# A diffusion layer on eight cores: the residual stream kept in an HBM scratch during the MLP, longer contractions, and no arithmetic on GpSimd there

## The chip, the cores and the metric

The kernel runs on the eight cores of one Trainium2 chip. Each pair of cores takes one of the four batch elements and each core of a pair one half of its 2048 tokens, so each core computes 1024 tokens of the output. The time is that of the slowest core, in device microseconds (us).

## The reference, cut to what matters

```python
D_MODEL = 2048; D_FF = 8192; BATCH = 4; SEQ = 2048     # float32

def hybrid_layer(...):                       # depth 1
    h = modulate(rmsnorm(x, g1), sh1, sc1)
    q, k, v, u = split_proj(h @ w_in)        # 12 query heads, 4 kv heads, 4 Fourier groups
    ...                                      # attention over 256 context + 2048 latent keys
    x = x + gt1 * (concat([attn, four]) @ w_out)
    h2 = modulate(rmsnorm(x, g2), sh2, sc2)
    a = relu(h2 @ w1)                        # (2048 -> 8192)
    x = x + gt2 * ((a * a) @ w2)             # (8192 -> 2048)
return rmsnorm(x, final_norm_g)
```

The case is about the last lines: the squared-ReLU MLP and the residual `x` to which it is added.

## The kernel before

Everything is held transposed: features on the 128 partitions, tokens along the free dimension, in two token groups `tg` of 512. The residual stream of a core, 16 feature tiles `d` by two token groups of [128, 512] in float32, is called `ACC(tg, d)` and lives in SBUF as the tiles `acc_0`, `acc_1` (tg 0) and `acc_2` (tg 1), 8 MB in all. The output projection (`w_out`) adds to it; the sum of its squares gives the second norm, whose result, in bf16, is `h_0`, `h_1`, `h_2`.

The MLP then runs as a list of units. The 8192 hidden features are 32 pairs of 256. The first two pairs (weights `wc`) and the second product of the last four pairs (weights `w2l`) are done plainly. All else uses a Strassen-Winograd scheme on 2x2 blocks: seven products take the place of eight. An `Up` unit makes the hidden activations of one pair: its 2x2 blocks are halves of the 2048 input features by the two feature tiles of the pair and by the two token groups, and each of its seven products is 8 matmuls deep, 56 matmuls of 128x128 by 128x512. A `Down` unit makes four output tiles, `(0, d)`, `(1, d)`, `(0, d+8)`, `(1, d+8)`, from one group of `kh` pairs: 7 x kh matmuls. The groups are `GROUPS = [6, 6, 6, 5, 5, 4]` pairs: after the Ups of a group (only those beyond the two plain pairs in the first) come its eight Down units; the last group of four is done plainly at the end by `stage_b`, followed by the final norm and the stores of the output.

A unit `n` has three PSUM banks, `P`, `Q`, `R`, of two sets that take turns, and two of four weight tiles `wr` (`WRAW`), each filled by one DMA on GpSimd's queue that casts float32 to bf16. `sums()` computes five sums of weight blocks on VectorE (three into `ws` tiles, two in place in `wr`). `first()` does two products, of which P is copied by ScalarE to a temporary `s` and Q added to it by VectorE. `mid()` does three products, with P and Q accumulating on; `last()` the remaining two, and it is issued after the next unit's `first()`, except at a turn from Up to Down, where it goes ahead of it since the Down unit needs what the last Up makes. After an Up pair VectorE also forms five sums of the activations (`a2_sums`, over the tiles `a_0` to `a_6`). A temporary comes from `temp()`, which hands out seven tiles in turn (`tt`, `bv`, `cf`, `sqa`).

In a Down unit `take_r` makes four scaled copies on ScalarE (`put`) and adds them to the residual on GpSimd, and `take_12`, `take_21`, `take_11`, `take_22` each add one scaled PSUM bank to a residual tile with one VectorE instruction (`scalar_tensor_tensor`, line 159, with the gate `modcol` or its negative `ng`):

```python
def put(self, acc, col, src, tmp):
    R.act(tmp, src, AF.Copy, scale=col)
    R.tt(acc, acc, tmp, ALU.add, eng='pool')
```

The weights of the last stage, `w2l`, go to parts of the `a` tiles and of `hs_a` that come free, in eight DMAs from the fourth-last unit on.

The order on each engine is not the order of the code: a recorder (`Rec`) collects all operations with the ranges that they read and write, a list scheduler with assumed durations, DMA rates and the priority of the code's order places them, and each engine then executes its own list in that order, with semaphore waits. In the profile most instructions therefore have the line of the recorder's helper: 116 is a matmul, 147 and 170 ScalarE, 156 a tensor_tensor of VectorE or GpSimd, 159 the scalar_tensor_tensor, 182 a DMA.

Of the kernel before, what the change touches and what calls it, by code (L numbers as in the profile page):

```python
# [14 lines left out]
D = 2048  # L15
# [16 lines left out]
class Rec:  # L32
# [47 lines left out]
    def add(self, eng, fn, reads=(), writes=(), dur=0.1, dma=None, nbytes=0, level=None, after=()):  # L80
        r = [x for a in reads for x in self.spans(a)]
        w = [x for a in writes for x in self.spans(a)]
# [338 lines left out]
GROUPS = [6, 6, 6, 5, 5, 4]  # L421
# [31 lines left out]
def build_program():  # L453
# [25 lines left out]
    ccsc_d = din("dft_ch", [128, 256])  # L479
    out_d = nc.dram_tensor("out", [2 * 16 * 128, 512], F32, kind="ExternalOutput").ap()  # L480

    with ExitStack() as st:
# [47 lines left out]
        def at(name, kb, shape, dt=F32):  # L530
# [526 lines left out]
        R.level = 3  # L1057
        h0, h21 = H20, H21[1]
# [20 lines left out]
        def a2_sums(j):  # L1079
            b11, b22, b12, b21, s1, s2, s3 = [A2[c][:, j, :] for c in range(7)]  # L1080
# [10 lines left out]
        for tg in range(2):  # L1091
            for p in range(2):
                for f in range(2):
# [3 lines left out]
                    squared(A2[((0, 3), (2, 1))[tg][f]][:, p, :], PS[b], TT[(0, 3, 6)[rot('tc', 3)]])  # L1097
# [4 lines left out]
        for p in range(2):  # L1102
            a2_sums(p)
# [347 lines left out]
```

How the kernel before makes its waits and increments, by code:

```python
        def run(name, eng):  # L375
            for op in per[name]:
                for kind, a, b, q in op['waits']:
                    if kind == 1:
                        eng.wait_ge(esem[a], self.sig[q])
                    else:
                        eng.wait_ge(dsem[a], b)
                ins = op['fn'](eng)
                if op['dma'] is not None:
                    ins.then_inc(dsem[op['dma']], 16)
                elif op['i'] in self.sig:
                    ins.then_inc(esem[name], 1)
            if name == 'sp':
                for k, v in self.dma_cnt.items():
                    if k.startswith('out'):
                        eng.wait_ge(dsem[k], v)
```

## Time and profile before

| | us |
|---|---|
| median of 3 runs | 1818.13 |
| lowest and highest of them | 1596.5, 1822.4 |
| the profiled execution | 1595.7 |
| its span, on its slowest core (2) | 1594.2 |
| spans of the eight cores | 1581.2 to 1594.2 |

| engine, core 2 | busy us | share |
|---|---|---|
| TensorE matmul (PE) | 1452.7 | 91% |
| VectorE (DVE) | 963.8 | 60% |
| ScalarE (ACT) | 803.8 | 50% |
| GpSimd (POOL) | 387.8 | 24% |

The span of a core is the time from its first to its last instruction; the time of the execution has 1.5 us more. An engine's busy time doesn't tell whether it is what the others wait for: that is in the waits and in the timeline. The MLP begins at 740 us with the matmuls of the `wc` tiles; its units end at 1524 us, where `stage_b` starts.

### The profile page before, as it was taken

Reading aid. Unit: us, or ns where it says so; the run is one execution under the profiler, and the core shown is the slowest. Engines: PE = TensorE matmul, PEld = TensorE weight load, DVE = VectorE, ACT = ScalarE, POOL = GpSimd, SP = SyncE. Lnnn points to the kernel's source line nnn. Section 1 sums busy time; section 2 is a strip of 40 time slices with the busy share of each in tenths; the row PEclk is TensorE's granted clock in tenths of the full one; section 3 lists DMA queues with packets and bytes.
Section 4 is the critical chain, followed back from the end, with each engine's and each line's share of the span. In section 5 each row is a group of like instructions: output and inputs, shape, how many; then the busy total and the mean of one; then the engine's idle time right before and its main releaser. Section 6 shows DMA issues by size and latency. Waiting matters only on the chain.

```text
span 1594.2 us, 29287 instructions; the slowest of 8 cores (1581.2 to 1594.2 us)
## 1 busy us (share of the span) xinstructions
PE 1452.7 (91%) x9931; PEld 752.4 (47%) x10103; DVE 963.8 (60%) x1715; ACT 803.8 (50%) x1706; POOL 387.8 (24%) x467
## 2 busy tenths in 40 slices
PE   0589998989999999999999999999999979979997
PEld 0244554456666666444444444444444434434447
DVE  0253658845445432254777677776776788679447
ACT  1055647567777787154543354334433433443478
POOL 1100010000000010322036304620661354056132
PEclk9989999999999999999999999999999989999999
DMA  9999997479557699005336544555455346446916
GB/s 208 187 192 236 207 166 133 81 128 159 109 95 135 122 189 233 10 14 93 50 56 97 88 92 71 92 91 85 71 87 91 55 67 101 82 58 86 155 21 212
DMA packets 47937, 179.57 MB, mean 113 GB/s; under 512 B 4656, under 2 KB 12208, under 8 KB 37040
## 3 DMA queue, kind: packets, MB, share of 16 engines
q0 software_dynamic: 33584, 139.65, 53.4%
q1 hardware_dynamic: 14208, 38.04, 7.4%
q8 instruction: 84, 1.38, 0.3%
q14 instruction: 61, 0.50, 0.1%
HBM read 308.92 MB, written 8.39 MB: 199 GB/s over the span
## 4 chain that ended last, share of the span: by engine, by line
PE 68%; DMA 19%; DVE 5%; issue 5%; ACT 2%; POOL 1%; another core or an unknown queue 0%; DVEq 0%; ACTq 0%; POOLq 0%; SPq 0%
PE ps L116 67%; DMA wr<-w 6%; DMA wada<-w_ada 5%; DMA xs<-xt 3%; DMA wadb<-w_ada 2%; DVE ws L156 2%; DMA wadm<-w_ada 2%; DVE acc L159 1%; DMA ropeq<-rope_q 1%; POOL acc L156 1%; PE ps L128 1%; DVE hf L156 0%; DVE tt L156 0%; POOL wr L182 0%
## 5 line engine op out<-in xcount | busy, mean ns | idle before, releaser
L147 ACT ACTIVATE pt<-ps 128x512 bf16<-128x512 f32 x432 | 224.0, 633 | 58.5 <-PE ps L116 58.1
L116 PE MATMUL ps<-a,wr 128*128 128x512 bf16 x880 | 204.1, 381 | 14.3 <-DVE acc L159 13.6
L182 POOL DMA_DIRECT2D wr<-w x140 | 76.8, 549 | 449.7 <-DVE tt L156 154.9
L159 DVE SCALAR_TENSOR_TENSOR acc<-ps,modcol,acc 128x512 f32<-128x512 f32 (+2 forms) x176 | 112.2, 650 | 119.0 <-PE ps L116 98.1
L116 PE MATMUL ps<-a,ws 128*128 128x512 bf16 x657 | 157.9, 386 | 21.9 <-DVE ws L156 20.6
L116 PE MATMUL ps<-v,pt 128*128 128x129 bf16 x1728 | 151.8, 220 | 2.7 <-issue 0.6
L116 PEld LDWEIGHTS ps<-a,wr 128*128 128x128 bf16 x896 | 87.5, 98 | 123.0 <-issue 21.1
L116 PEld LDWEIGHTS ps<-v,pt 128*128 128x128 bf16 x1728 | 123.4, 98 | 39.7 <-issue 2.4
L116 PE MATMUL ps<-qT,kT 128*128 128x512 bf16 x385 | 135.3, 381 | 1.0 <-issue 0.2
L156 DVE TENSOR_TENSOR ws<-wr,wr 128x1024 bf16<-128x1024 bf16 (+2 forms) x140 | 105.4, 791 | 44.7 <-DMA wr<-w 41.4
L156 POOL TENSOR_TENSOR acc<-acc,tt 128x512 f32<-128x512 f32 x91 | 118.2, 1309 | 14.7 <-ACT tt L147 13.9
L116 PEld LDWEIGHTS ps<-a,ws 128*128 128x128 bf16 x672 | 65.6, 99 | 105.8 <-issue 32.9
L116 PE MATMUL ps<-h,wr 128*128 128x512 bf16 x472 | 109.6, 380 | 0.5
L116 PE MATMUL ps<-h,ws 128*128 128x512 bf16 x469 | 107.9, 379 | 0.9 <-DVE sqa L156 0.3
L156 DVE TENSOR_TENSOR wr<-wr,wr 128x1024 bf16<-128x1024 bf16 (+2 forms) x140 | 103.8, 778 | 1.0
L116 PE MATMUL ps<-wq,h 128*128 128x512 bf16 x370 | 91.9, 385 | 2.5 <-DVE yk L159 1.7
L116 PE MATMUL ps<-qT,wo 128*128 128x512 bf16 x375 | 87.5, 379 | 0.5
L147 ACT ACTIVATE tt<-tt 128x512 f32<-128x512 f32 x69 | 43.4, 628 | 86.3 <-DVE tt L156 86.2
L156 DVE TENSOR_TENSOR ws<-wr 128x1024 bf16<-128x1024 bf16 (+2 forms) x70 | 72.9, 1041 | 17.5 <-DMA wr<-w 16.9
L116 PE MATMUL ps<-wv,h 128*128 128x512 bf16 x244 | 68.2, 427 | 15.6 <-DMA wv<-w_v 10.6
L147 ACT ACTIVATE sqn<-acc 128x512 bf16<-128x512 f32 (+2 forms) x93 | 42.9, 478 | 76.9 <-DVE acc L159 76.8
L170 ACT COPY tt<-ps 128x512 f32<-128x512 f32 x60 | 34.7, 579 | 89.1 <-PE ps L116 89.1
(240 smaller groups left out, 2382.7 us busy)
## 6 DMA issues: line engine op xcount, KB each, us to landing
wr<-w POOLq DMA_DIRECT2D x60, 512.0 KB, 6.3
wadb<-w_ada POOLq DMA_DIRECT2D x25, 1024.0 KB, 11.7
xs<-xt SPq DMA_DIRECT2D x18, 1024.0 KB, 15.3
wr<-w POOLq DMA_DIRECT2D x48, 384.0 KB, 5.2
wr<-w POOLq DMA_DIRECT2D x32, 320.0 KB, 4.5
wada<-w_ada POOLq DMA_DIRECT2D x8, 1024.0 KB, 36.0
wada<-w_ada POOLq DMA_DIRECT2D x16, 512.0 KB, 13.5
wo<-w_out POOLq DMA_DIRECT2D x8, 1024.0 KB, 11.8
```

The lines of the kernel that those rows point to most:

```text
L116: ins = e.matmul(o, lhsT=l, rhs=r, start=a, stop=b, skip_group_check=more)
L128: ins = e.transpose(out=o, in_=i_, identity=ident)
L147: self.add('act', lambda e: e.activation(out=out, in_=in_, func=func, scale=scale, **kw), reads, writes, dur, level=level)
L156: self.add(eng, lambda e: e.tensor_tensor(out=out, in0=a, in1=b, op=op), [a, b], [out], dur, level=level)
L159: self.add('dve', lambda e: e.scalar_tensor_tensor(out=out, in0=a, scalar=s, in1=b, op0=op0, op1=op1), [a, b] + ([] if isinstance(s, float ...
L170: self.add('act', lambda e: e.copy(out=out, in_=in_), [in_], [out], 0.051 + self.fs(in_) / 1.2e3, level=level)
L182: return self.add(q, lambda e: e.dma_start(out=out, in_=in_), [] if load else [in_], [out] if load else [], 0.55 if q == 'pool' else 0.45, ...
```

## The change

Before the MLP the eight quarters of the residual (4 tiles each, 1 MB) are stored by DMAs of SyncE's queue to a scratch in HBM, `mid`. Each Down unit fetches its four residual tiles from there with four DMAs of 256 KB (`fetch`, into the tiles `ar`, two sets of four) and stores them back with four others (`keep`), all on SyncE's queue; the last group of Downs fetches them straight to where the last stage wants them (`accf`) and stores nothing. `take_r` is now four VectorE instructions that add the scaled bank R and the temporary `s` to the fetched tiles; ScalarE's four copies and GpSimd's four additions are gone. The SBUF that this frees makes the groups longer, `[10, 9, 9, 4]`: 24 Down units in place of 40, with the same number of matmuls. The Ups of the last four pairs now come ahead of the last group of Downs, with activations in places of their own (`PL`), so that the stage after the Downs follows them directly; there are two turns from Up to Down in place of five. `w2l` is loaded by seven DMAs, four of them during the last Downs and three (10 of the 16 blocks) behind the last unit.

```diff
-GROUPS = [6, 6, 6, 5, 5, 4]
+GROUPS = [10, 9, 9, 4]
...
+    mid_d = nc.dram_tensor("mid", [32 * 128, 512], F32, kind="Internal").ap()
...
-        HSA = at('hs_a', 44, [8, 512], BF16)
-        HS1 = at('hs_1', 52, [8, 512], BF16)
-        HS2 = at('hs_2', 36, [8, 512], BF16)
+        HSA = at('hs_a', 144, [8, 512], BF16)
+        HS1 = at('hs_1', 152, [8, 512], BF16)
+        HS2 = at('hs_2', 176, [8, 512], BF16)
...
-        A2 = [at('a2_%d' % i, kb, [KH, 512], BF16) for i, kb in enumerate((76, 82, 88, 94, 100, 60, 66))]
+        A2 = [at('a2_%d' % i, kb, [KH, 512], BF16) for i, kb in enumerate((76, 86, 96, 42, 108, 118, 128))]
...
+        W2L = [at('wl_%d' % i, kb, [n, 8, 128], BF16) for i, (kb, n) in enumerate(((140, 2), (200, 2), (138, 1), (190, 1), (76, 4), (86, 4), (108, 2)))]
+        AR = [at('ar_%d' % i, 60 + 2 * i, [512]) for i in range(8)]
...
         R.level = 3
+        for tg in range(2):
+            for d in (8, 12, 0, 4):
+                src = A1[:, d:d + 4, :] if tg else A0[d // 8][:, d % 8:d % 8 + 4, :]
+                R.dma('sp', mid_d[(tg * 16 + d) * 128:(tg * 16 + d + 4) * 128, :].rearrange("(g p) n -> p g n", p=128),
+                      src, 'ms%d_%d' % (tg, d), load=False, far=((), range(tg * 16 + d, tg * 16 + d + 4)))
...
         class Down(Unit):
...
-            def put(self, acc, col, src, tmp):
-                R.act(tmp, src, AF.Copy, scale=col)
-                R.tt(acc, acc, tmp, ALU.add, eng='pool')
+            def fetch(self):
+                for i, (tg, d) in enumerate(self.spots):
+                    t = tg * 16 + d
+                    R.dma('sp', self.at[i], rows(mid_d, t), 'al%d' % t if self.end else 'ar%d' % (self.n % 2 * 4 + i), far=((t,), ()))
...
+            def take(self, i, c, src):
+                R.stt(self.at[i], src, self.col[c], self.at[i], ALU.mult, ALU.add)
 
             def take_r(self):
-                self.put(ACC(1, d), ncol(d), self.s, temp())
...
+                self.take(0, 0, self.R)
+                self.take(3, 1, self.R)
+                self.take(1, 2, self.s)
+                self.take(2, 3, self.s)
 
             def take_12(self):
-                self.take(ACC(1, self.d), gcol(self.d), self.P)
+                self.take(1, 0, self.P)
+                self.keep(1)
...
-            turn = i and spec[0] is Down and units[i - 1][0] is Up
+            turn = i and spec[0] is Down and units[i - 1][0] is Up and i < len(units) - 8
...
-            for k in {len(units) - 4: (0, 1), len(units) - 3: (2, 3, 4), len(units) - 2: (5, 6)}.get(i, ()):
-                load_late(k, [sent])
+            if i >= len(units) - 5 and i < len(units) - 1:
+                load_late(i - len(units) + 5, [sent])
             u.mid()
             if i + 1 < len(units):
                 made[i + 1].sums()
+                if units[i + 1][0] is Down:
+                    made[i + 1].fetch()
             load(i + 2, 0)
+        for k in (4, 5, 6):
+            load_late(k)
         made[len(units) - 1].last()
```

How the order of three engines changes. GpSimd, at the end of the first Downs, before: four additions to the residual stand between the weight DMAs of each unit.

```order
L182 DMA wr_169<-w 128x1536
L182 DMA wr_172<-w 128x1536
L156 TENSOR_TENSOR acc_157<-acc_157,sqa 128x512
L156 TENSOR_TENSOR acc_156<-acc_156,bv 128x512
L156 TENSOR_TENSOR acc_155<-acc_155,tt_184 128x512
L156 TENSOR_TENSOR acc_157<-acc_157,cf 128x512
L182 DMA wr_171<-w 128x1536
L182 DMA wr_170<-w 128x1536
```

The same queue in the changed kernel, where the first Downs begin:

```order
L182 DMA wr_169<-w 128x2560
L182 DMA wr_172<-w 128x2048
L182 DMA wr_171<-w 128x2560
L182 DMA wr_170<-w 128x2560
L182 DMA wr_172<-w 128x2560
```

Only DMAs are left, of 10 blocks (2560 elements a partition) in place of 6.

VectorE, one Down unit before: five weight sums of 768 elements, the addition of Q to `s` and four takes.

```order
L156 TENSOR_TENSOR ws_176<-wr_171 128x768
L156 TENSOR_TENSOR ws_174<-wr_169,wr_170 128x768
L156 TENSOR_TENSOR ws_175<-wr_170,wr_169 128x768
L156 TENSOR_TENSOR wr_170<-wr_169,wr_170 128x768 x2
L156 TENSOR_TENSOR cf<-cf,ps 128x512
L159 SCALAR_TENSOR_TENSOR acc_155<-ps,ng,acc_155 128x512
L159 SCALAR_TENSOR_TENSOR acc_157<-ps,ng,acc_157 128x512
L159 SCALAR_TENSOR_TENSOR acc_157<-ps,modcol,acc_157 128x512
L159 SCALAR_TENSOR_TENSOR acc_156<-ps,modcol,acc_156 128x512
```

And in the changed kernel:

```order
L156 TENSOR_TENSOR ws_176<-wr_171 128x1280
L156 TENSOR_TENSOR ws_174<-wr_169,wr_170 128x1280
L156 TENSOR_TENSOR ws_175<-wr_170,wr_169 128x1280
L156 TENSOR_TENSOR wr_170<-wr_169,wr_170 128x1280 x2
L156 TENSOR_TENSOR cf<-cf,ps 128x512
L159 SCALAR_TENSOR_TENSOR ar_198<-cf,ng,ar_198 128x512
L159 SCALAR_TENSOR_TENSOR ar_201<-ps,ng,ar_201 128x512
L159 SCALAR_TENSOR_TENSOR ar_199<-cf,ng,ar_199 128x512
L159 SCALAR_TENSOR_TENSOR ar_204<-ps,ng,ar_204 128x512
L159 SCALAR_TENSOR_TENSOR ar_197<-ps,modcol,ar_197 128x512
L159 SCALAR_TENSOR_TENSOR ar_200<-ps,modcol,ar_200 128x512
L159 SCALAR_TENSOR_TENSOR ar_198<-ps,modcol,ar_198 128x512
```

The takes go to the fetched tiles `ar`, and there are eight of them in a unit, two of which read the temporary (`cf` here) and not a bank.

SyncE's queue between the loads of the residual and the stores of the output, before:

```order
L182 DMA acc_156<-xo 128x2048 [waits s_dve]
L182 DMA acc_155<-xo 128x2048 [waits d_adb1_0,s_pe]
L182 DMA acc_157<-xo 128x2048 [waits s_pe] x3
L182 DMA acc_155<-xo 128x2048 [waits d_adb0_0,s_pe]
L182 DMA out<-acc_155 128x4x512 [waits s_dve]
```

Nothing stands between them.

The same queue in the changed kernel, in the middle of the first Downs (`s_dve` is a wait for VectorE, `d_as0` to `d_as7` one for the end of the store of that residual tile):

```order
L182 DMA mid<-ar_197 128x512 [waits s_dve]
L182 DMA mid<-ar_200 128x512 [waits s_dve]
L182 DMA mid<-ar_202 128x512 [waits s_dve]
L182 DMA ar_197<-mid 128x512 [waits d_as0]
L182 DMA mid<-ar_203 128x512 [waits s_dve]
L182 DMA ar_200<-mid 128x512 [waits d_as3]
L182 DMA ar_202<-mid 128x512 [waits d_as5]
L182 DMA ar_203<-mid 128x512 [waits d_as6]
```

Each tile is stored when its last take is done, and the same SBUF tile is fetched anew, for the next unit but one, when its store has ended; fetches stand in the queue behind stores that wait for VectorE.

## Rows read from the trace of the kernel before

**Rows 1.** Windows: length, busy us by engine, clock, DMA share, GB/s; the MLP.

```profile
740.00:826.00 86.00, 84.84 (x388) 38.54 (x395) 59.92 (x102) 49.65 (x81) 6.50 (x11) 1.00 0.30 46
826.00:1524.00 698.00, 652.96 (x2926) 291.30 (x2983) 511.07 (x761) 277.81 (x453) 276.09 (x294) 0.99 0.53 86
1524.00:1594.00 70.00, 61.98 (x560) 43.23 (x563) 43.03 (x83) 54.97 (x142) 25.69 (x25) 0.96 0.37 121
```

**Rows 2.** Windows of 50 us inside the MLP; columns as above.

```profile
1200.00:1250.00 50.00, 49.79 (x229) 22.65 (x233) 32.27 (x59) 23.24 (x40) 5.05 (x10) 1.00 0.51 88
1250.00:1300.00 50.00, 40.68 (x177) 17.79 (x180) 38.50 (x54) 19.55 (x33) 24.45 (x24) 0.93 0.41 59
1300.00:1350.00 50.00, 43.88 (x192) 19.12 (x195) 45.04 (x54) 16.02 (x25) 25.60 (x26) 0.97 0.55 86
...
1400.00:1450.00 50.00, 42.19 (x183) 18.48 (x185) 40.75 (x55) 19.23 (x30) 33.77 (x32) 0.93 0.44 62
1450.00:1500.00 50.00, 44.84 (x197) 19.62 (x199) 35.92 (x46) 18.14 (x29) 20.19 (x25) 0.97 0.82 124
```

**Rows 3.** Timeline of PE: start, length, operation, count [idle before, releaser].

```profile
776.71 1.89 PE L116 MATMUL ps<-hs_a,wr 128*128 128x512 bf16 x8
...
788.80 1.89 PE L116 MATMUL ps<-hs_a,wr 128*128 128x512 bf16 x8
...
830.49 2.75 PE L116 MATMUL ps<-a,wr 128*128 128x512 bf16 x12 [1.77 <-DVE acc L159]
...
1284.37 4.08 PE L116 MATMUL ps<-a,ws 128*128 128x512 bf16 x10 [6.29 <-DVE ws L156]
```

**Rows 4.** Waits of PE, 740 to 1524 us: us in total, times, longest.

```profile
PE ps L116 <- DVE ws L156: 20.6, 9, 6.3
PE ps L116 <- DVE acc L159: 15.6, 12, 3.6
...
PE ps L116 <- DMA wr<-w: 2.3, 1, 2.3
```

**Rows 5.** Timeline of DVE; columns as for PE.

```profile
1262.84 5.30 DVE L156 TENSOR_TENSOR wr<-wr,wr 128x640 bf16<-128x640 bf16 x1
...
1270.05 2.07 DVE L159 SCALAR_TENSOR_TENSOR acc<-ps,modcol,acc 128x512 f32<-128x512 f32 x3
```

**Rows 6.** Timeline of POOL over the same moments.

```profile
1262.84 1.29 POOL L156 TENSOR_TENSOR acc<-acc,tt 128x512 f32<-128x512 f32 x1
1264.07 1.28 POOL L156 TENSOR_TENSOR acc<-acc,sqa 128x512 f32<-128x512 f32 x1
1265.30 1.26 POOL L156 TENSOR_TENSOR acc<-acc,tt 128x512 f32<-128x512 f32 x1
1266.53 1.25 POOL L156 TENSOR_TENSOR acc<-acc,cf 128x512 f32<-128x512 f32 x1
```

**Rows 7.** Groups by form: 830 to 1480 us, then Ups (1205 to 1250).

```profile
L159 DVE SCALAR_TENSOR_TENSOR acc<-ps,modcol,acc 128x512 f32<-128x512 f32 x80 | 58.2, 745 | 30.3 <-POOL acc L156 20.1 <-PE ps L116 10.2
...
L156 DVE TENSOR_TENSOR wr<-wr,wr 128x640 bf16<-128x640 bf16 x32 | 32.4, 1048 | 0.2
...
L156 DVE TENSOR_TENSOR wr<-wr,wr 128x1024 bf16<-128x1024 bf16 x8 | 5.1, 685 | 0.0
```

**Rows 8.** DMA queues: packets, MB, share; 826 to 1480, then 1560 to 1594.

```profile
q0 software_dynamic: 17756, 52.68, 50.1%
...
q1 hardware_dynamic: 8448, 8.39, 73.8%
...
out<-acc SPq DMA_DIRECT2D x8, 256.0 KB, 2.6
```

**Rows 9.** The two weight DMAs of 1 MB (tile wc).

```profile
L182 POOL DMA_DIRECT2D wc<-w x2: 530/550/570, 711.8 to 712.9; - x2
...
DMA to landing us min/median/max: 11.1/12.6/14.2
```

**Rows 10.** DMA share in 40 slices of the span (page).

```profile
DMA  9999997479557699005336544555455346446916
```

More of the change, by code:

```diff
@@ L77, in spans, with add @@
         return out
-    def add(self, eng, fn, reads=(), writes=(), dur=0.1, dma=None, nbytes=0, level=None, after=()):
-        r = [x for a in reads for x in self.spans(a)]
-        w = [x for a in writes for x in self.spans(a)]
+    def add(self, eng, fn, reads=(), writes=(), dur=0.1, dma=None, nbytes=0, level=None, after=(), far=((), ())):
+        r = [x for a in reads for x in self.spans(a)] + [('D', i, i + 1) for i in far[0]]
+        w = [x for a in writes for x in self.spans(a)] + [('D', i, i + 1) for i in far[1]]
         i = len(self.ops)
@@ L1077, in squared, with slots, a2_sums @@
             R.act(dst, tmp, AF.Square)
-        def a2_sums(j):
-            b11, b22, b12, b21, s1, s2, s3 = [A2[c][:, j, :] for c in range(7)]
+        def slots(j):
+            return [A2[c][:, j, :] for c in range(7)]
+        def a2_sums(of):
+            b11, b22, b12, b21, s1, s2, s3 = of
             R.tt(s2, b11, b12, ALU.add)
@@ L1102, in build_program @@
         for p in range(2):
-            a2_sums(p)
+            a2_sums(slots(p))
         class Unit:
@@ new lines, in __init__ @@
+                self.end = g == len(GROUPS) - 2
+                self.at = [ACCF(*k) if self.end else AR[n % 2 * 4 + i] for i, k in enumerate(self.spots)]
+                self.col = [f(d + 8 * i) for f in (gcol, ncol) for i in range(2)]
+            def fetch(self):
+                for i, (tg, d) in enumerate(self.spots):
+                    t = tg * 16 + d
+                    R.dma('sp', self.at[i], rows(mid_d, t), 'al%d' % t if self.end else 'ar%d' % (self.n % 2 * 4 + i), far=((t,), ()))
@@ new lines, in keep @@
+            def keep(self, i):
+                if not self.end:
+                    tg, d = self.spots[i]
+                    t = tg * 16 + d
+                    R.dma('sp', rows(mid_d, t), self.at[i], 'as%d' % (self.n % 2 * 4 + i), load=False, far=((), (t,)))
+            def take(self, i, c, src):
+                R.stt(self.at[i], src, self.col[c], self.at[i], ALU.mult, ALU.add)
+            def take_r(self):
+                self.take(0, 0, self.R)
+                self.take(3, 1, self.R)
+                self.take(1, 2, self.s)
+                self.take(2, 3, self.s)
@@ L1214, in take_22 @@
             def take_22(self):
[L1215 removed]
+                self.take(3, 3, self.Q)
+                self.keep(3)
         units = []
@@ L1219, in build_program @@
         for g, size in enumerate(GROUPS):
+            plain = g == len(GROUPS) - 1
             for j in range(size):
                 if base + j > 1:
-                    units.append((Up, base + j, j))
+                    units.append((Up, base + j, PL[4 * j:4 * j + 4] if plain else slots(j)))
             base += size
-            if g < len(GROUPS) - 1:
+            if g < len(GROUPS) - 2:
                 units += [(Down, g, d, size) for d in range(8)]
+        units += [(Down, len(GROUPS) - 2, d, GROUPS[-2]) for d in range(8)]
         made = {}
@@ L1232, in load @@
                 return made[i].load(half)
-        late_w = [(0, 3, flat(A2[4][:, 0:6, :])), (3, 6, flat(A2[5][:, 0:6, :])), (6, 9, flat(A2[6][:, 0:6, :]))]
-        late_w += [(9 + c, 10 + c, flat(A2[c][:, 4:6, :])) for c in range(4)] + [(13, 16, flat(HSA[:, 0:6, :]))]
         def load_late(k, after=()):
-            lo, hi, dst = late_w[k]
-            R.dma('pool', dst, w2l_d[:, 1024 * lo:1024 * hi], 'wl%d' % k, after=after)
+            lo = sum(w.shape[1] for w in W2L[:k])
+            n = W2L[k].shape[1]
+            R.dma('pool', W2L[k].rearrange("p d j n -> p (d j n)"), w2l_d[:, 1024 * lo:1024 * (lo + n)], 'wl%d' % k, after=after)
         for i in range(2):
```

68 lines of the change are left out of this document (33 added, 35 removed).

## The prediction

> **What bounds the kernel now.** I read the windows of the MLP first, then the timeline and the waits of PE, then what VectorE and GpSimd did in the longest of them, last the DMA queues. In the MLP's units, 740 to 1524 us, PE is busy 84.8 + 653.0 of 784 us [rows 1]. One Up unit, 56 matmuls, takes 788.80 - 776.71 = 12.09 us where nothing disturbs it [rows 3], 0.216 us a matmul. The units have 128 + 30 x 56 + 8 x 7 x 28 = 3376 matmuls, 729 us at that pace. So 784 - 729 = 55 us are lost, and that is all that a change which keeps the matmuls can win there. The reader should see where they lie: a stretch of Ups loses next to nothing (49.79 of 50 us), the windows with the Downs of 5 pairs lose 9.3 and 7.8 us of 50 in idle time, and in these the granted clock falls to 0.93 [rows 2]: after an idle time of 6.29 us, 10 matmuls take 4.08 us in place of 2.16 [rows 3], so part of them ran at the lower of the two levels, 1.2 GHz.
>
> PE waits 20.6 us for weight sums (`ws`) and 15.6 us for the takes (`acc`), which must empty a bank [rows 4]. Both are VectorE's. Why is it late? At 1262.84 us a weight sum of 640 elements takes 5.30 us [rows 5], and at the same 1262.84 GpSimd begins four additions to the residual, back to back until 1267.78 [rows 6]. The sums in place of this form average 1048 ns in the Downs, while those of 1024 elements take 685 ns in the Ups, where GpSimd adds nothing [rows 7]. A bf16 sum on VectorE is held up by GpSimd's additions, for as long as they follow one another. That is the bound that the change touches.
>
> **What goes.** (1) The additions, and with them the 36.2 us of waits for VectorE. (2) The slow clock behind them: (1 - granted clock) x 50 us is 3.5, 1.5 and 3.5 us in the windows from 1250, 1300 and 1400 [rows 2], 8.5 us. (3) The wait of 2.3 us for a weight DMA and the 1.5 us of slow clock in the window from 1450 [rows 2, 4]: there `w2l` is loaded between the weights, at a DMA share of 0.82. Now one DMA of it comes in each of the last units, of a kind that needs less, and I count 3.8 us as won. ScalarE's four copies go too; nothing on PE waits for them. Together 48.5 us. Of the 55 the other 6.6 are small waits and the matmuls' own jitter, and I leave them.
>
> **What comes on VectorE.** A Down unit of 10 pairs has 70 matmuls, 15.1 us of PE; of 9 pairs 63, 13.6 us. VectorE has in it five sums of 1280 elements: 8 sums of 1024 took 5.1 us [rows 7], 0.64 each, so 0.80 each and 4.0 in all; one addition, 0.7; and eight takes in place of four, at the pace of three in 2.07 us [rows 5] 5.5 us. That is 10.2 of 15.1 us, 67% (9.8 of 13.6, 72%, with 9 pairs). In the Ups, VectorE is busy 32.27 of 50 us, 65%, and PE waits for nothing [rows 2]. So the added takes are hidden as long as nothing blocks VectorE. At a turn VectorE does cost: the first one has a wait of 1.77 us [rows 3]. Two turns are left; I give back 2 us each, 4 in all (0 to 10).
>
> **What comes on the DMA engines.** The weight queue moved 52.68 MB at a share of 50.1% of 654 us, that is 6.2 us of all 16 engines for each MB that it writes [rows 8]. SyncE's queue moved 8.39 MB in 73.8% of 34.2 us, 3.0 us a MB [rows 8]. A Down unit of 10 pairs needs 1.31 MB of weights (8.2 us) and 1.05 MB of residual each way (6.3 us): 14.5 us in the 15.1 that PE takes. Of 9 pairs: 7.3 + 6.3 = 13.6 of 13.6. The last group, which stores nothing, needs 7.3 + 3.2 and 1.2 for `w2l`. So in the first 16 Downs the DMA engines, at 0.53 now [rows 1], are filled to 96 and 100%. This is the new risk, and it is carried by what is fetched ahead: a weight DMA has 8 to 12 products (17 to 26 us) between its issue and its use, a fetch of the residual about 10 us, behind two stores. Then VectorE has three more products before PE needs the bank. A 256 KB transfer lands in 2.6 us when alone [rows 8]. What it lands in beside a full weight queue the trace doesn't show. From below the cost is 0, since the demand still fits; from above, were every MB of residual as dear as one of weights, a unit of 10 would need 8.2 + 13.1 = 21.3 us and one of 9 20.4, 8 x 6.2 + 8 x 6.8 = 104 us too much. I take 6 us, near the lower end, since the tail's row is of the very transfer (same queue, 2 KB rows, all cores at once) and the average fits.
>
> The eight stores of the residual before the MLP, 8.39 MB or 25 us of DMA time, fall where the DMA share is 0 for two slices, 80 us [rows 10], and stand ahead of nothing on SyncE's queue until the first fetch. I cost them at nothing; if the last of them were late it would be the first `a2_sums`, whose tiles lie on `acc_2`, and 5 us at most.
>
> Behind the last unit: 2.6 MB of `w2l` are issued in the order 2, 4, 4 blocks, the one needed first last. Before, two DMAs of 1 MB issued at 711.8 and 712.9 landed within 14.2 us [rows 9], 2 MB in 15.3. So 2.6 MB land some 18.5 us after the end of product m1. PE has two products of that unit's middle, two of its end (4 x 1.9) and six blocks (6 x 8 x 0.216 = 10.4) before it needs them, 18.1 us. I take 1 us (0 to 6).
>
> **The sum**, against the profiled execution's own 1595.7 us (span 1594.2 and 1.5 around it; 0.8 under the lowest of the three timed runs, and far under their median of 1818.13, since two of the three took over 1818; the forecast is for an execution like the profiled one): 1595.7 - 48.5 + 4 + 6 + 1 = 1558.2, taken as 1558. That is 2.4% less. A measurement of this kernel can tell about 2% from no change, 1564 us, so the forecast lies close to that line.
>
> One rule of the Trainium skill speaks against the change. The page SBUF — State Buffer, section The DMA setup-cost knee, gives a transfer of 256 KiB 224 GB/s where one of 1 MiB gets 341, because each pays about 2 us that don't scale. The rows above have 332 GB/s for a queue whose transfers were 256 KB to 1 MB, because several were under way. By the rule 2.1 MB of residual take 9.4 us, a unit of 10 needs 17.5 us in 15.1, and the time comes to that of the second rival.
>
> **Rivals.** (a) *The additions weren't the cause.* Then VectorE stays late for want of time, with four more takes. Against it: 5.30 us for one sum, to the moment of GpSimd's run. Time: 36.2 + 8.5 stay, 1558 + 45 = 1603. 5%.
>
> (b) *The DMA engines become the bound, in part*: the residual costs not 3.0 but 4.5 us a MB beside weights. Then a unit of 10 needs 8.2 + 9.4 = 17.6 us, one of 9 16.7: 8 x 2.5 + 8 x 3.1 = 45 us in place of my 6, 1597; half of that, 1577. For it: no margin at all in the second group. Against: the price per MB of either queue. 27%, from 1566 to 1600.
>
> (c) *Slower: the residual's transfers run one after the other.* SyncE's queue is in order, and each fetch waits for a store, which waits for VectorE. Eight transfers of 2.6 us are 20.8 us a unit. If they don't overlap, VectorE waits for each unit's tiles, PE for the banks: 8 x (20.8 - 15.1) + 8 x (20.8 - 13.6) = 103 us, 1655. It decides from 15.1 / 8 = 1.9 us a transfer on. Against it: the order has up to four of them back to back. 11%.
>
> (d) *Everything fits*: no DMA cost, no turn cost, 1547 or just under. 5% beyond the range below it.
>
> The forecast itself, 1547 to 1566, has 52%. From 1564 up to 1600, (a) in part and (b), about a third. So: faster by over 2% 0.56, within 2% 0.32, slower 0.12. The range of 8 in 10 is 1546 to 1600: it leaves out (c), most of (a) and what lies under 1546.
>
> **What would show it.** In the profile after: bf16 sums of 1280 elements near 0.85 us in the Downs, none over 1.5; no additions on GpSimd between the second norm and the last stage; waits of PE for `ws` and for the takes (now `ar`) under 10 us together; a granted clock of 1.00 through the Downs; a DMA share over 0.9 in the first 16 Downs. If PE waits there for VectorE, and VectorE for DMAs of `ar` or `wr`, it is (b) or (c): (c) if the DMA share stays under 0.8, (b) if it is 0.99. The forecast fails if a transfer of 256 KB lands in over 6 us, or if VectorE's order puts a late weight sum ahead of the takes.

## The result

The changed kernel takes 1553.4 us (median of four executions, 1549.6 to 1556.6), 0.971 of the kernel before, with a 95% interval of 0.966 to 0.976: 2.9% less, where 2.4% was forecast. The ratios, and the medians in the table of experiments, are of undisturbed executions only, while the medians of before (1818.13 as shown ahead, and 1710.1 with a fourth run) have disturbed ones among them. The profiled execution took 1549.6 us with a span of 1548.0, on core 1, against 1595.7 and 1594.2.

The windows of the MLP after; the units now end at 1477 us. Columns as in [rows 1].

```profile
740.00:826.00 86.00, 85.96 (x400) 38.78 (x397) 60.91 (x102) 47.69 (x78) 4.74 (x9) 1.00 0.54 114
826.00:1477.00 651.00, 645.87 (x2986) 291.17 (x2985) 430.70 (x697) 165.99 (x282) 53.82 (x102) 1.00 0.71 148
1477.00:1548.00 71.00, 62.40 (x564) 42.84 (x562) 43.58 (x83) 53.70 (x140) 25.61 (x25) 0.97 0.49 148
```

The first `wc` matmul starts at 741.0 us and `stage_b` at 1476.7, so the units take 735.7 us, where their matmuls at 0.216 us each need 729. Of the 55 us that were lost there 7 are left, 48 are won. What lies ahead and behind changed by little: the start is 0.8 us later, and the last stage has 71 us in place of 70 [rows 1]. The saving is all in the units.

The waits of PE in the units, which answer to [rows 4]:

```profile
PE ps L116 <- DVE ws L156: 2.2, 3, 1.0
PE ps L116 <- DVE ar L159: 1.7, 1, 1.7
PE ps L116 <- DVE cf L156: 0.5, 1, 0.5
PE ps L116 <- DVE tt L156: 0.4, 1, 0.4
```

The waits for weight sums fell from 20.6 us to 2.2, those for takes from 15.6 to 1.7 (the tiles are now `ar`). To see why, read the same groups by form as in [rows 7], of 860 to 1480 us.

```profile
L159 DVE SCALAR_TENSOR_TENSOR ar<-ps,modcol,ar 128x512 f32<-128x512 f32 x64 | 45.9, 746 | 17.9 <-PE ps L116 17.6
...
L156 DVE TENSOR_TENSOR ws<-wr,wr 128x1280 bf16<-128x1280 bf16 x16 | 12.5, 821 | 18.5 <-DMA wr<-w 18.5
L156 DVE TENSOR_TENSOR wr<-wr,wr 128x1280 bf16<-128x1280 bf16 x16 | 12.4, 819 | 0.0
```

A sum of 1280 elements takes 820 ns; the sums of 640 took 1048. A take, which reads one of its two large operands from PSUM, costs what it did with additions beside it: 746 ns, before 745. Four windows of the Downs, two of each of the first two groups, columns as in [rows 2]:

```profile
900.00:950.00 50.00, 50.00 (x233) 22.70 (x232) 33.27 (x48) 1.76 (x3) 3.70 (x7) 1.00 0.91 210
950.00:1000.00 50.00, 50.00 (x234) 22.65 (x232) 28.42 (x42) 5.34 (x9) 3.16 (x6) 1.00 0.87 208
1100.00:1150.00 50.00, 50.00 (x232) 22.52 (x231) 34.74 (x53) 3.19 (x6) 3.70 (x7) 1.00 0.88 197
1150.00:1200.00 50.00, 48.26 (x223) 21.27 (x221) 31.15 (x47) 1.76 (x3) 3.17 (x6) 1.00 0.93 221
```

PE is busy all of 50 us, but for 1.7 us near the end of the second group, the granted clock stays at 1.00, the higher of its two levels (2.4 GHz), and the DMA share is 0.87 to 0.93, where the windows from 1250, 1300 and 1400 us had 0.41 to 0.55 before [rows 2]. The queues from 860 to 1225 us, to be read with [rows 8] (the last column of an issue is the median time to landing):

```profile
q0 software_dynamic: 7628, 30.63, 50.1%
q1 hardware_dynamic: 18092, 32.96, 28.6%
...
mid<-ar SPq DMA_DIRECT2D x64, 256.0 KB, 8.0
ar<-mid SPq DMA_DIRECT2D x56, 256.0 KB, 4.3
...
wr<-w POOLq DMA_DIRECT2D x13, 640.0 KB, 8.1
```

30.63 MB of weights in 50.1% of 365 us are 6.0 us a MB, 32.96 MB of residual in 28.6% 3.2 us a MB. The prediction had 6.2 and 3.0.

### The profile page after: what moved, and what is told of

It reads as the page before. It is cut to its first block, busy times and chain, and to the rows that moved or that the text cites. A ratio compares the mean times of both kernels' runs of the same rounds, so it can differ in the third digit from the quotient of the medians.

```text
span 1548.0 us, 28760 instructions; the slowest of 8 cores (1538.7 to 1548.0 us)
## 1 busy us (share of the span) xinstructions
PE 1456.1 (94%) x10103; PEld 752.5 (49%) x10103; DVE 883.5 (57%) x1651; ACT 688.6 (44%) x1530; POOL 163.5 (11%) x274
## 3 DMA queue, kind: packets, MB, share of 16 engines
q1 hardware_dynamic: 41472, 88.38, 17.6%
## 4 chain that ended last, share of the span: by engine, by line
PE 79%; DMA 14%; issue 2%; DVE 2%; ACT 2%; POOL 0%; DVEq 0%; ACTq 0%; POOLq 0%; SPq 0%
PE ps L116 78%; DMA wr<-w 5%; DMA wada<-w_ada 5%; DMA wadm<-w_ada 2%; DMA xs<-xt 1%; DMA ropeq<-rope_q 1%; PE ps L128 1%; DMA wl<-w2l 1%; ACT sqx L147 0%; DVE ws L156 0%; DVE wr L156 0%; ACT h L147 0%; DVE xs L156 0%; POOL wr L182 0%; DVE hf L156 0%
## 5 line engine op out<-in xcount | busy, mean ns | idle before, releaser
L116 PE MATMUL ps<-qT,kT 128*128 128x512 bf16 x432 | 151.9, 381 | 0.3
L116 PE MATMUL ps<-a,ws 128*128 128x512 bf16 x672 | 150.2, 379 | 1.8 <-DVE ws L156 1.2
L182 POOL DMA_DIRECT2D wr<-w x108 | 57.1, 529 | 663.3 <-DVE tt L156 275.1
L156 DVE TENSOR_TENSOR ws<-wr,wr 128x1024 bf16<-128x1024 bf16 (+2 forms) x108 | 74.2, 728 | 80.0 <-DMA wr<-w 78.9
L170 ACT COPY tt<-ps 128x512 f32<-128x512 f32 x50 | 28.7, 575 | 179.5 <-PE ps L116 179.5
L116 PEld LDWEIGHTS ps<-h,ws 128*128 128x128 bf16 x480 | 46.8, 98 | 58.3 <-issue 2.3
L116 PEld LDWEIGHTS ps<-h,wr 128*128 128x128 bf16 x480 | 46.8, 98 | 57.5 <-issue 1.3
L156 DVE TENSOR_TENSOR wr<-wr,wr 128x1024 bf16<-128x1024 bf16 (+2 forms) x108 | 73.9, 725 | 0.2
L159 DVE SCALAR_TENSOR_TENSOR accf<-ps,modcol,accf 128x512 f32<-128x512 f32 (+2 forms) x96 | 52.7, 570 | 33.2 <-PE ps L116 32.5
L156 DVE TENSOR_TENSOR a<-a,a 128x512 bf16<-128x512 bf16 x140 | 51.7, 421 | 34.2 <-ACT a L147 34.2
```

Of the source, the lines that this page charges most:

```text
L116: ins = e.matmul(o, lhsT=l, rhs=r, start=a, stop=b, skip_group_check=more)
L156: self.add(eng, lambda e: e.tensor_tensor(out=out, in0=a, in1=b, op=op), [a, b], [out], dur, level=level)
L159: self.add('dve', lambda e: e.scalar_tensor_tensor(out=out, in0=a, scalar=s, in1=b, op0=op0, op1=op1), [a, b] + ([] if isinstance(s, float ...
L170: self.add('act', lambda e: e.copy(out=out, in_=in_), [in_], [out], 0.051 + self.fs(in_) / 1.2e3, level=level)
```

## The experiments

Twelve runs: ten edits, one of them run a second time, and the changed kernel again. "Excess" is the time that VectorE's bf16 weight sums took beyond their durations without any hindrance (482, 551, 685, 753 and 820 ns for 640, 768, 1024, 1152 and 1280 elements, from runs without additions): the count times the difference of the means, summed over the forms, on the slowest core (in the first run with takes on VectorE on core 2), from 826 us to the end of the units. "PE's waits" are those of PE for VectorE from 740 us to the end of the profile's units or just behind it.

| run | median us | ratio to before (95%) | GpSimd's additions | excess us | PE's waits us |
|---|---|---|---|---|---|
| before, profiled | 1595.7 | 1 | 160 | 84 | 40 |
| changed, again | 1553.7 | 0.971 (0.968 to 0.974) | 0 | 0 | 4 |
| before, takes on VectorE | 1553.7 | 0.975 (0.969 to 0.981) | 0 | 0 | 7 |
| the same again | 1557.9 | 0.974 (0.971 to 0.976) | 0 | 0 | 7 |
| before, additions left out | 1549.2 | 0.974 (0.968 to 0.980) | 0 | 0 | 6 |
| before, GpSimd writes only | 1553.7 | 0.972 (0.968 to 0.977) | 160 memsets | 0 | 3 |
| before, half moved | 1574.3 | 0.983 (0.979 to 0.988) | 80 | 36 | 26 |
| changed, additions back | 1557.2 | 0.977 (0.970 to 0.985) | 96 | 10 | 19 |
| changed, additions twice | 1589.6 | 0.993 (0.990 to 0.995) | 192 | 64 | 36 |
| changed, short groups | 1667.1 | 1.046 (1.042 to 1.050) | 0 | 0 | 76 |
| changed, fetched twice | 1592.4 | 0.994 (0.992 to 0.997) | 0 | 0 | 35 |
| changed, groups 10, 10, 8 | 1557.9 | 0.974 (0.971 to 0.977) | 0 | 0 | 7 |
| changed, last weights in order | 1559.5 | 0.975 (0.972 to 0.979) | 0 | 0 | 11 |

The row of the run with additions back rests on two executions, of 1551.6 and 1562.8 us. The runs were made on several chips, so the ratios, each to the kernel before on the same chip, compare better than the medians.

### The changed kernel again

> The changed kernel itself, beside the others on one chip: 1550 to 1557 us.

It came to 1553.7 us, a ratio of 0.971 (0.968 to 0.974), with an excess of 0 and 4 us of waits for VectorE: the result repeats.

### Only the additions moved

```diff
             def put(self, acc, col, src, tmp):
-                R.act(tmp, src, AF.Copy, scale=col)
-                R.tt(acc, acc, tmp, ALU.add, eng='pool')
+                R.stt(acc, src, col, acc, ALU.mult, ALU.add)
```

> The kernel before, with only the four additions of a Down unit moved from GpSimd (and their four copies on ScalarE) to four takes on VectorE; groups, turns and the residual in SBUF stay. Theory A (GpSimd's additions hold VectorE's bf16 sums): no hold-ups, sums of 640 near 0.49 us, but VectorE now needs 8.6 of 9.1 us in a unit of 6 pairs and 8.2 of 7.6 in one of 5, some 11 us too much and more by bunching: 1565 to 1580 us. Theory B (the gain comes of fewer and longer units and fewer turns): nothing won, 1596 or more, since VectorE has more to do.

It gave 1553.7 us, a ratio of 0.975 against the whole change's 0.971, and 11 us less than I had allowed. It was run again beside the changed kernel:

> The kernel before with only the additions moved to takes on VectorE, again, beside the changed kernel on one chip. If the scratch and the long groups bring nothing of their own: within 4 us of the changed kernel. If they bring what is left of VectorE's load: the changed kernel 5 to 10 us faster.

It came to 1557.9 against 1553.7 us. This kernel has no scratch and no long groups, 40 Downs and five turns, so theory B, by which it would have won nothing, is refuted. What the scratch and the long groups add to it is some 4 us, and the two intervals (0.971 to 0.976, 0.968 to 0.974) overlap, so the times alone don't show it. The profile of this second run has a place for about that much. Two windows inside the 5-pair Downs, columns as in [rows 2]:

```profile
1262.00:1285.00 23.00, 21.82 (x101) 9.40 (x100) 23.00 (x42) 1.30 (x3) 3.18 (x6) 1.00 0.52 82
1285.00:1308.00 23.00, 22.49 (x104) 9.76 (x103) 23.00 (x42) 1.76 (x3) 3.18 (x6) 1.00 0.55 90
```

and the timeline of PE there:

```profile
1279.14 2.32 PE L116 MATMUL ps<-a,wr 128*128 128x512 bf16 x10 [0.17 <-DVE acc L159]
...
1287.03 2.32 PE L116 MATMUL ps<-a,wr 128*128 128x512 bf16 x10 [0.17 <-DVE acc L159]
...
1294.91 2.32 PE L116 MATMUL ps<-a,wr 128*128 128x512 bf16 x10 [0.17 <-DVE acc L159]
```

VectorE is busy 23.00 of 23 us: here it is the bound. A unit comes every 7.88 us where its 35 matmuls need 7.56, some 0.3 us too much in each of the 16 units of 5 pairs, 5 us. I had expected 11 us, counting 0.69 us a take; the takes follow each other at 0.66, as VectorE's timeline in the same run shows:

```profile
1292.70 2.72 DVE L159 SCALAR_TENSOR_TENSOR acc<-ps,modcol,acc 128x512 f32<-128x512 f32 x4
1295.34 0.48 DVE L156 TENSOR_TENSOR ws<-wr 128x640 bf16<-128x640 bf16 x1
1295.74 0.89 DVE L156 TENSOR_TENSOR ws<-wr,wr 128x640 bf16<-128x640 bf16 x2
1296.54 0.88 DVE L156 TENSOR_TENSOR wr<-wr,wr 128x640 bf16<-128x640 bf16 x2
```

### The additions left out

The edit drops the second line of `put` alone. GpSimd's additions are left out, so the residual lacks the terms of bank R and of `s`.

> The kernel before, with GpSimd's four additions of a Down unit left out (ScalarE's copies stay; the residual lacks these terms); all else as it was, 40 Down units and five turns. Theory A: the waits for VectorE (36 us) and the slow clock behind them (8.5 us) go: 1551 us, within 5, and sums of 640 at 0.49 us. Theory B: 1590 or more.

The time is 1549.2 us, the excess 0. The forms in that run, 830 to 1460 us:

```profile
L156 DVE TENSOR_TENSOR ws<-wr,wr 128x640 bf16<-128x640 bf16 x32 | 14.4, 488 | 11.8 <-DMA wr<-w 9.2 <-PE ps L116 2.5
L156 DVE TENSOR_TENSOR wr<-wr,wr 128x640 bf16<-128x640 bf16 x32 | 14.3, 483 | 0.0
```

A sum in place takes 483 ns where it took 1048 [rows 7]. Nothing but GpSimd's additions was taken away, ScalarE's copies were still there, and the whole saving came.

An addition can cost time in a second way: a take must wait for an addition to the same residual tile. VectorE stood idle for that 20.1 us before [rows 7], and this edit ends it too, as do moving the additions and the memsets below. The trace of the kernel before tells the two apart. The ten longest waits of PE for VectorE (1.3 to 6.3 us, 28.9 of the 40 us together) each end behind sums that had been held, for example the wait of 3.59 us at 1303.6 us behind a pair of sums of 4.73 us, which takes 0.88 alone. In none of them does a take's wait for GpSimd stand last. How much the waits of 20.1 us add to PE's shorter ones no run separates.

### What of GpSimd's work does it

```diff
                 R.act(tmp, src, AF.Copy, scale=col)
-                R.tt(acc, acc, tmp, ALU.add, eng='pool')
+                R.add('pool', lambda e: e.memset(tmp, 0.0), [], [tmp], 1.2)
```

The additions are left out here too, and a memset of the temporary stands in the place of each.

> The kernel before with each addition on GpSimd replaced by a memset of the same temporary, 128 x 512 in float32 (the residual lacks these terms): GpSimd writes as much, and reads nothing. If any work of GpSimd on SBUF holds VectorE's two-input sums: near the kernel before, 1580 or more. If only GpSimd's reads do: as with the additions left out, 1549, sums of 640 at 0.49 us.

The ratio is 0.972, and there is no excess in a single form. From the timeline of all engines there, GpSimd's and VectorE's rows:

```profile
1279.63 0.89 DVE L156 TENSOR_TENSOR ws<-wr,wr 128x640 bf16<-128x640 bf16 x2 [0.73 <-DMA wr<-w]
1279.84 0.53 POOL L1193 MEMSET tt<- 128x512 f32 x1 [3.38 <-ACT tt L147]
...
1280.44 0.89 DVE L156 TENSOR_TENSOR wr<-wr,wr 128x640 bf16<-128x640 bf16 x2
```

A memset begins 0.2 us after two sums did, and the two take 0.89 us, as always. So it is not GpSimd's work as such; what the additions have and the memsets lack is first of all the reading of SBUF. The Trainium skill has this rule on the page SBUF — State Buffer, section Who interferes with whom: a VectorE instruction with two SBUF inputs contends with a GpSimd instruction that reads SBUF, not with one that only writes it. The trace agrees, with 84 us of excess beside 160 additions and none beside 160 memsets. The memset is shorter, though, 0.53 us against 1.28, and does no arithmetic, so that the reading is the cause rests on the rule and these rows together: no run made GpSimd write, without reading, for as long as the additions took.

### How much of it reaches TensorE

Two of the four additions moved, in the kernel before (those of `s` stay on GpSimd):

```diff
-                self.put(ACC(0, d), gcol(d), self.R, temp())
-                self.put(ACC(1, d + 8), gcol(d + 8), self.R, self.r)
+                self.take(ACC(0, d), gcol(d), self.R)
+                self.take(ACC(1, d + 8), gcol(d + 8), self.R)
```

> The kernel before with two of the four additions of a unit (those of the bank R) made takes on VectorE, and two left on GpSimd: 34% of a unit of 5 pairs, 28% of one of 6. If the share decides: an excess of the sums of 10 to 25 us, few waits of PE, 1555 to 1565. If any addition beside a sum is enough: half of the gain, 1575.

It came to 1574.3 us (0.983 against the whole change's 0.971): the second of the two expectations, somewhat over half of the gain. A held sum in it, VectorE's and GpSimd's rows of its timeline:

```profile
1294.13 0.90 DVE L156 TENSOR_TENSOR ws<-wr,wr 128x640 bf16<-128x640 bf16 x2 [0.34 <-DMA wr<-w]
1294.75 1.40 POOL L156 TENSOR_TENSOR acc<-acc,tt 128x512 f32<-128x512 f32 x1 [3.32 <-ACT tt L147]
...
1294.94 3.38 DVE L156 TENSOR_TENSOR wr<-wr,wr 128x640 bf16<-128x640 bf16 x2
```

Two sums of 0.89 us together take 3.38. Beside them are two additions, at 1294.75 and at 1296.69 us, with the issue of a weight DMA between them: two are enough for that.

All four back on GpSimd, in the changed kernel:

```diff
+            def put(self, i, c, src, tmp):
+                R.act(tmp, src, AF.Copy, scale=self.col[c])
+                R.tt(self.at[i], self.at[i], tmp, ALU.add, eng='pool')
+
             def take_r(self):
-                self.take(0, 0, self.R)
...
+                self.put(1, 2, self.s, temp())
+                self.put(2, 3, self.s, self.s)
+                self.put(0, 0, self.R, temp())
+                self.put(3, 1, self.R, self.r)
```

> The changed kernel, with the additions of R and s to the fetched tiles back on GpSimd, behind four scaled copies on ScalarE; long groups, two turns and the scratch stay. Theory A: sums of 1152 and 1280 elements average over 1.2 us in the Downs, waits of PE for VectorE return, softened since VectorE has more room in a long unit (7.4 of 15.1 us): 1560 to 1585. Theory B: 1553, as the changed kernel.

The two executions took 1551.6 and 1562.8 us, a ratio (0.970 to 0.985) that can't be told from the changed kernel's. The excess is only 10 us, though 96 additions stand in the Downs; the sums of 1280 average 991 and 898 ns on core 6, far from the 1200 that I expected. Theory A named what holds the sums, but this run says something that it left out: with the long units the additions cost little even on GpSimd, so either half of the change alone, the takes on VectorE or the scratch with its long units, gives most of the saving (the second by the middle of a wide interval). Why is the excess so small? VectorE's and GpSimd's rows of the timeline of one unit of 10:

```profile
889.70 1.56 DVE L156 TENSOR_TENSOR ws<-wr,wr 128x1280 bf16<-128x1280 bf16 x2 [2.05 <-DMA wr<-w]
...
891.17 1.55 DVE L156 TENSOR_TENSOR wr<-wr,wr 128x1280 bf16<-128x1280 bf16 x2
...
894.30 1.26 POOL L156 TENSOR_TENSOR ar<-ar,tt 128x512 f32<-128x512 f32 x1 [0.40 <-ACT tt L147]
...
895.53 1.26 POOL L156 TENSOR_TENSOR ar<-ar,cf 128x512 f32<-128x512 f32 x1
...
897.72 1.26 POOL L156 TENSOR_TENSOR ar<-ar,tt 128x512 f32<-128x512 f32 x1 [0.42 <-ACT tt L147]
898.95 1.26 POOL L156 TENSOR_TENSOR ar<-ar,sqa 128x512 f32<-128x512 f32 x1
...
901.27 0.75 DVE L159 SCALAR_TENSOR_TENSOR ar<-ps,modcol,ar 128x512 f32<-128x512 f32 x1 [1.41 <-PE ps L116]
902.81 0.82 DVE L156 TENSOR_TENSOR ws<-wr 128x1280 bf16<-128x1280 bf16 x1 [0.79 <-DMA wr<-w]
```

The sums run from 889.7 to 892.7 us, the additions from 894.3 to 900.2, the next sum starts at 902.8: they don't meet. In a unit of 15 us the sums have their place and the additions theirs; in one of 7.6 us they fall on each other. To tell that from the share of time in which GpSimd adds, each addition was made twice (so that the residual holds these terms twice):

> The changed kernel with the additions back on GpSimd, each made twice (the residual then holds these terms twice): 8 additions of 1.28 us in a Down unit, 10.2 of 15.1 or 13.6 us, 68 to 75% of the unit, as the four were in the units of 5 pairs before (68%). If it is the share of time in which GpSimd adds that sets the hold-up of VectorE's sums: their excess over the undisturbed durations (9.5 us in all with single additions, 82 us in the kernel before) rises over 40 us, and the time to 1575 to 1600. If long units are safe as such: within 8 us of the run with single additions.

The time is 1589.6 us, the excess 64 us, PE's waits for VectorE 36: with runs of twice the length the sums and the additions meet in the long units too. Most of the excess is in the first sum of a unit, which stands right behind the takes. The rows are of that sum, of a later one, and of takes:

```profile
L156 DVE TENSOR_TENSOR ws<-wr 128x1152 bf16<-128x1152 bf16 x16 | 44.5, 2781 | 14.8 <-DMA wr<-w 14.7
...
L156 DVE TENSOR_TENSOR wr<-wr,wr 128x1280 bf16<-128x1280 bf16 x16 | 14.3, 929 | 0.2
...
L159 DVE SCALAR_TENSOR_TENSOR ar<-ps,modcol,ar 128x512 f32<-128x512 f32 x32 | 23.9, 748 | 56.3 <-POOL ar L156 53.3 <-PE ps L116 3.0
```

The first sum takes 2781 ns (1152 elements, 753 alone), a later one 929 (1280 elements, 820 alone). But the excess is not all that the doubled additions cost: VectorE's takes also stood idle until GpSimd had added to the same tile, 53.3 us in this form and 74 in all the takes together (23 with single additions), and 25 of PE's 36 us are waits for takes. The 36 us that this run loses against the changed kernel are of both, and it doesn't part them. Long units are not safe as such. The share of the time in which GpSimd adds isn't the measure of the excess either: with half moved GpSimd adds for 28 to 34% of a unit, in the run with additions back for 34 to 38%, and the excess is 36 us there and 10 here. What fits all the runs is whether runs of additions and sums stand side by side, in the order of the kernel. That is read from the timelines of one or two units, not tested by an order made for it.

### The price of the scratch

```diff
-GROUPS = [10, 9, 9, 4]
-KH = max(GROUPS)
+GROUPS = [6, 6, 6, 5, 5, 4]
+KH = 10
```

> The changed kernel with the groups of before, 6, 6, 6, 5, 5 and 4 pairs: 40 Down units, each with its fetches and stores. Theory A with the price list of the DMA queues (5.9 us of all engines a MB of weights, 3.2 a MB of residual, as in the profile after): a unit of 6 needs 11.3 us of DMA in 9.1, one of 5 10.5 in 7.6, the last group 7.2 in 7.6; 24 x 2.2 + 8 x 2.9 = 76 us, 1629 us, DMA share 0.95 or more in the first 32 Downs. Were the residual's traffic hidden at any length, VectorE's load alone (as in the run with the takes on VectorE) would give 1565 to 1580.

It came to 1667.1 us, 113 more than the changed kernel. Windows of the Downs, and PE's waits:

```profile
1050.00:1100.00 50.00, 42.14 (x167) 17.69 (x168) 33.97 (x55) 3.92 (x7) 4.22 (x8) 0.88 0.85 205
...
1200.00:1250.00 50.00, 42.04 (x168) 17.02 (x168) 34.51 (x57) 2.34 (x4) 4.02 (x8) 0.90 0.90 229
```

```profile
PE ps L116 <- DVE ar L159: 52.5, 17, 6.8
PE ps L116 <- DVE ws L156: 18.5, 13, 2.4
PE ps L116 <- DMA wr<-w: 7.6, 3, 3.2
```

The DMA share is 0.85 to 0.90, not the 0.95 that I expected, and the time is 38 us over my price list's. The clock accounts for about that: the mean granted clock of this core is 0.964 where the changed kernel had 0.987, 2.3% of 1666 us, 38 us; it falls to 0.88 and 0.90 in these windows, behind waits of up to 6.8 us. The price list itself (76 us of DMA time over what PE takes) holds: from 740 to 1595 us, where the units end, PE is idle for 84 us, and it was idle for 5 in the changed kernel's units. PE waits for VectorE and not for a DMA: a weight sum that waits for its weights (134 us in all on VectorE) holds back the takes queued behind it. Short groups and the scratch don't go together: that is what the long groups are for.

Fetching each residual tile of the first two groups twice:

```diff
                     R.dma('sp', self.at[i], rows(mid_d, t), 'al%d' % t if self.end else ..., far=((t,), ()))
+                    if not self.end:
+                        R.dma('sp', self.at[i], rows(mid_d, t), 'ar%d' % (self.n % 2 * 4 + i), far=((t,), ()))
```

> The changed kernel with each residual tile of the first two groups of Downs fetched twice, 1 MB more a unit. If the DMA engines' time is what counts (5.9 and 3.2 us a MB): a unit of 10 needs 17.6 us in 15.1, one of 9 16.9 in 13.6; 8 x 2.5 + 8 x 3.3 = 46 us more, 1599 us, with a DMA share near 1. If there is more room than the prices say: under 1575. If the queue's order is what counts (each fetch waits for a store): more than 1620.

It came to 1592.4 us, 39 more than the changed kernel; 46 were expected. DMA share and clock in two windows, one in each group:

```profile
950.00:990.00 40.00, 31.48 (x129) 12.81 (x128) 21.48 (x31) 1.17 (x2) 2.11 (x4) 0.91 0.99 253
...
1150.00:1200.00 50.00, 43.32 (x187) 18.63 (x186) 26.01 (x38) 1.76 (x3) 3.08 (x6) 0.93 0.95 236
```

With some 3.3 us of DMA time more in a unit the share is 0.99 and 0.95, and nearly all of the gain is gone (0.994). This is what rival (b) of the prediction described: one MB more in each unit is all that stands between the changed kernel and it.

### Two tries at a better version

```diff
-GROUPS = [10, 9, 9, 4]
+GROUPS = [10, 10, 8, 4]
```

> The changed kernel with groups of 10, 10, 8 and 4 pairs: the shortest Downs are those that store nothing. By the queues' prices a unit of 10 needs 14.3 us of DMA in 15.1, the last group's of 8 some 10.5 in 12.1; the one group at 100% (9 pairs, 13.6 of 13.6) is gone. If the waits of PE in the second group (about 4 us in the profile after) come of the DMA share: 3 to 5 us less than the changed kernel. If they come of the turn: the same.

It came to 1557.9 us, 4 more than the changed kernel on the same chip and not 3 to 5 less; the intervals overlap. The tight group of 9 went, PE's waits didn't: one of 2.8 us stands in the last group of Downs, one of 3.3 before the last stage. The expectation failed.

```diff
-        ... ((140, 2), (200, 2), (138, 1), (190, 1), (76, 4), (86, 4), (108, 2))
+        ... ((140, 2), (200, 2), (138, 1), (190, 1), (108, 2), (86, 4), (76, 4))
```

> The changed kernel with the three late DMAs of the last weights in the order in which they are needed (2 blocks, then 4, then 4, each to the place that comes free in that order). The prediction's term for them was 1 us; the profiles show a wait of PE for them of 0.4 to 2.3 us on some cores. Expected: that wait gone on all cores, and 0 to 3 us less than the changed kernel, 1549 to 1554 us, which is within what the rounds can tell. If the wait stays, it is the queue's volume and not its order.

The wait for the last weights is gone on all eight cores. The time is 1559.5 us all the same. Up to the last units this kernel issues the same instructions in the same order on every engine, yet PE's waits for VectorE in the Downs are 11 us in its profile and 4 to 5 in the two of the changed kernel; weights of 640 KB landed in 9.1 us there, in 8.1 and 8.4 here. This job ran on another chip than the others. So differences of 5 us between such runs need not come of the edits, and neither of the two versions is shown better or worse.

## Why the prediction was right, and where not

**The cause** was named rightly: GpSimd's additions hold VectorE's sums. The 36.2 us of PE's waits, the 8.5 us of slow clock behind them and the 3.8 us around `w2l` were to bring 48.5 us, of which the sum gave 11 back; 48 us were won in the units with all that came back already taken off. PE's waits for VectorE went from 40 to 5 us. The run without additions gives 0.974, the one with memsets 0.972. One sentence was too strong: that a sum is held for as long as the additions follow one another. Some are, like the one of 5.30 us; others run between two additions, as the last section shows. And the prediction took the end of the additions as the only way to win these 36.2 us. The run with additions back has them in the long units and is not clearly slower than the changed kernel, so the long units alone would have won most of it too.

**The step that failed** is what the sum gave back and left in place. It kept 17.6 us of loss: 6 for the DMA engines, 4 for the turns, 1 for the last weights, and the 6.6 of small waits and jitter, put at "I leave them" without a reason. In the profile 7.1 us of it came:

- The DMA term, 6 us, measured 3.4: PE's waits in the second group of Downs, where the margin was put at nil. They are one of 1.7 us for a take at 1210 us and 1.7 at 1170 to 1187 for sums and an addition. The first group, put at 96%, has none.
- The turns, 4 us, measured 1.5, at 1227 and 1235 us.
- The small waits and jitter, 6.6 us, measured 1.8: of 55 us lost 6.7 remain, and 4.9 of them are the waits just named.
- The last weights, 1 us (0 to 6), measured 0.4 on the slowest core, up to 2.3 on others.

These 10.5 us too much, less some 2 us by which the start and the last stage grew, which the sum didn't have, are the difference between 1558 and the profiled 1549.6. The sizes rest on one profile; the kernel with the last weights in order, the same up to its last units, had 11 us of such waits on another chip. So 10 us for turns and DMA engines together was at the upper end of what these kernels show, and not out of reach. The base of the sum was the profiled execution's 1595.7 us, and the 2.4% hold against that base alone: against the median of 1818.13 a time of 1558 would be 14% less, which no run bears out.

**A sign of being wrong that was itself wrong:** "The forecast fails if a transfer of 256 KB lands in over 6 us". The stores landed in 8.0 us and the forecast stood. The fetches landed in 4.3, and VectorE waited for none of them. The 2.6 us "when alone" was read where SyncE's own queue filled 73.8% of the engines' time [rows 8], so it wasn't a transfer alone either.

**What comes on VectorE** was right: 67 to 72% of a Down unit, measured 33.27 and 34.74 of 50 us where a window has mostly Downs. That eight takes fit so well is due to the long groups; in a unit of 5 VectorE is full. What the prediction didn't see is that this costs only 5 us.

**The prices** of the DMA queues, 3.0 and 6.2 us a MB, were right to 7%, and the range's upper end, by rival (b), is what one more MB a unit made true (1592.4 against 1597).

**Rival (a)**, that the additions weren't the cause, is refuted. **Rival (c)**, that the residual's transfers run one after the other, didn't occur: stores land in 8.0 us and fetches in 4.3, and a unit of 15 us has four of each; one after the other they would take 49 us. They overlap. The Trainium skill's page SBUF — State Buffer, section The DMA setup-cost knee, gives a rate for 256 KiB by which 2.1 MB of residual would cost an estimated 9.4 us a unit. It was no guide here: at the 3.2 us a MB measured it is 6.7.

What stays open: why a store lands in twice the time of a fetch of the same size, whether the order of sums and additions alone, in short units, would have been enough, and how much the takes' waits for GpSimd's additions cost by themselves.

## What to carry to other kernels

When two engines work on SBUF at the same time, look at the durations of one form of instruction in a stretch where the other engine is silent and in one where it works: 482 against 1048 ns tells the cause here, before any wait does. First try the smallest edit that takes the work off the other engine; here one line gave 2.5% and the whole change 2.9%, which two intervals that overlap don't tell apart. And put it back into the changed kernel: here that showed that the other half of the change alone would have given most of the saving too. Traffic that is added to a full-length pipeline is priced in DMA time per unit of work, from the share and the bytes of each queue: 14.5 of 15.1 us was fine, 17.6 was not.

## What the runs showed of the hardware beyond that

- A bf16 sum on VectorE that meets a run of GpSimd's additions is held in one of two ways. It may wait for the whole run: 5.30 us beside four additions, to the end of the fourth [rows 5, 6]. Or it gets in between two of them, and the next addition takes longer. VectorE's and GpSimd's rows of the run with additions twice, a sum of 0.82 us alone and additions of 1.25:

```profile
894.46 1.26 POOL L156 TENSOR_TENSOR ar<-ar,bv 128x512 f32<-128x512 f32 x1
...
895.61 2.02 DVE L156 TENSOR_TENSOR ws<-wr 128x1280 bf16<-128x1280 bf16 x1 [0.26 <-DMA wr<-w]
895.69 3.06 POOL L156 TENSOR_TENSOR ar<-ar,tt 128x512 f32<-128x512 f32 x2
```

  The sum ends at 897.6 us, a microsecond before the two additions do, and these take 3.06 us in place of 2.5. What decides between the two ways no run shows. The page SBUF — State Buffer of the Trainium skill, section Who interferes with whom, says of VectorE's two-port modes that whoever issues first has the shared ports for its whole instruction and the other is fully blocked; the second way looks like that, instruction by instruction, and the first goes beyond it.
- 80 additions that stand beside such sums cost 36 us of excess, 96 that stand mostly apart from them 10.
- Stores of 256 KB to HBM landed in 8.0 us and fetches in 4.3 beside the weight queue, at a DMA share of 0.9; with the fetches doubled 9.8 and 5.9.
